# Joining weights of the first three attention pairs brought to the free axis through DRAM, in a hybrid decoder kernel

## The reference

```python
def dilated_attention(q, k, v):
    outs = [dilated_branch(q, k, v, w, d) for (w, d) in DILATED_BRANCHES]
    ms = jnp.stack([m for _, m, _ in outs])      # the maximum of each branch
    ls = jnp.stack([l for _, _, l in outs])      # the sum of its exponentials
    os_ = jnp.stack([o for o, _, _ in outs])
    wts = ls * jnp.exp(ms - jnp.max(ms, axis=0, keepdims=True))
    o = jnp.einsum('gbhs,gbhsd->bhsd', wts, os_) / jnp.sum(wts, axis=0)[..., None]
    return o
```

## Time and profile before

| | |
|---|---|
| median of 3 runs | 2058.66 us |
| the profiled execution | 2058.07 us |
| its span | 2056.3 us |
| PE busy | 2044.2 us, 99% |
| DVE, ACT, POOL busy | 66%, 44%, 44% |
| DMA share of the attention stretch (240 to 440 us) | 0.1 to 0.3 |

### The profile page before, as it was taken

How to read it: one execution, slowest core, us unless ns; L and a number is a source line. 1 busy time by engine, 2 the same in 40 slices (tenths; PEclk the granted TensorE clock), 3 DMA queues, 4 the chain that set the end, 5 groups by cost and what they waited for, 6 DMA issues and landing times.

```text
span 2056.3 us, 26348 instructions
## 1 busy us (share of the span) xinstructions
PE 2044.2 (99%) x10180; PEld 1695.3 (82%) x10180; DVE 1349.2 (66%) x1708; ACT 901.8 (44%) x1268; POOL 898.0 (44%) x467
## 2 busy tenths in 40 slices
PE   9999999999999999999999999999999999999998
PEld 7888888888888888888888888888888888888887
DVE  6668766747866555566999314538756556567987
ACT  4221565825544444443435420225544444454445
POOL 3322122233887777750003423345877877730002
PEclk9999999999999999999999999999999999999999
DMA  5110111133222222129982211113321222249872
GB/s 182 42 62 31 53 44 40 42 124 123 93 93 76 78 93 92 63 93 349 377 306 73 78 36 31 52 41 133 113 93 63 92 92 74 81 153 388 303 281 83
DMA packets 102534, 242.29 MB, mean 118 GB/s; under 512 B 12329, under 2 KB 18826, under 8 KB 102410
## 3 DMA queue, kind: packets, MB, share of 16 engines
q1 hardware_dynamic: 100538, 235.87, 32.3%
q10 hardware_dynamic: 1872, 4.74, 0.6%
HBM read 202.79 MB, written 35.68 MB: 116 GB/s over the span
## 4 chain that ended last, share of the span: by engine, by line
PE 94%; DMA 2%; DVE 1%; SPq 1%; POOL 0%; issue 0%; ACT 0%; POOLq 0%; DVEq 0%
PE ps L1508 13%; PE ps L1506 13%; PE ps L1507 13%; PE ps L991 6%; PE ps L994 6%; PE ps L997 6%; PE ps L1540 6%; PE ps L1542 6%; PE ps L1543 6%; PE ps L1221 2%; PE ps L1223 2%; PE ps L1222 2%; PE ps L1611 1%; PE ps L1613 1%; PE ps L1612 1%; PE ps L1363 1%
## 5 line engine op out<-in xcount | busy, mean ns | idle before, releaser
L696 POOL TENSOR_TENSOR w_hi<-w_raw,ones 128x1024 fp32r<-128x1024 f32 x52 | 103.5, 1990 | 664.5 <-PE ps L997 223.7
L1506 PE MATMUL ps<-t_hi,w_hi 128*128 128x512 f32 x672 | 261.4, 389 | 0.0
L1507 PE MATMUL ps<-t_lo,w_hi 128*128 128x512 f32 x672 | 261.4, 389 | 0.0
L1508 PE MATMUL ps<-t_hi,w_lo 128*128 128x512 f32 x672 | 261.4, 389 | 0.0
L760 POOL TENSOR_TENSOR w_lo<-w_sum,w_hi 128x1024 fp32r<-128x1024 f32 x84 | 248.3, 2958 | 14.1 <-ACT w_hi L2825 14.1
L1540 PE MATMUL ps<-d_hi 128*128 128x512 f32 (+1 forms) x632 | 242.3, 383 | 0.1
L1543 PE MATMUL ps<-d_hi,d_lo 128*128 128x512 f32 (+1 forms) x632 | 241.6, 382 | 0.0
L1542 PE MATMUL ps<-d_lo,d_hi 128*128 128x512 f32 (+1 forms) x632 | 241.6, 382 | 0.0
L760 POOL TENSOR_TENSOR w_lo<-w_raw,w_hi 128x1024 fp32r<-128x1024 f32 x84 | 158.0, 1881 | 159.8 <-ACT w_hi L2825 145.8
L1506 PE MATMUL ps<-act_hi,w_hi 128*128 128x512 f32 x504 | 196.1, 389 | 0.0
L1507 PE MATMUL ps<-act_lo,w_hi 128*128 128x512 f32 x504 | 196.1, 389 | 0.0
(11 more groups left out here) (335 smaller groups left out, 4342.8 us busy)
## 6 DMA issues: line engine op xcount, KB each, us to landing
w_raw<-w_up SPq DMA_DIRECT2D x44, 1024.0 KB, 4.9
d_ring<-w_dn SPq DMA_DIRECT2D x146, 256.0 KB, 7.6
d_ring<-g_kept SPq DMA_DIRECT2D x124, 256.0 KB, 9.1
g_kept<-gst SPq DMA_DIRECT2D x44, 512.0 KB, 3.6
w_raw<-w_in SPq DMA_DIRECT2D x24, 512.0 KB, 3.6
chain_a<-g_kept SPq DMA_DIRECT2D x44, 256.0 KB, 8.6
x_kept<-x SPq DMA_DIRECT2D x16, 512.0 KB, 9.2
x<-x_kept SPq DMA_DIRECT2D x16, 512.0 KB, 9.9
```

Of the source, the lines that this page charges most:

```text
L1506: pe.matmul(out, wh, bh, start=(fresh and j == 0), stop=False, skip_group_check=True)
L1507: pe.matmul(out, wh, bl, start=False, stop=False, skip_group_check=True)
L1508: ins = pe.matmul(out, wl, bh, start=False, stop=(j == 3), skip_group_check=True)
```

## The change

For pairs 0 to 2 the weights `a_part` (16 KB) are written to a DRAM buffer of 32 rows by 128 positions, element by element (one `factors_out` per pair), and read back (`factors_in`, two DMAs per chunk, one for each head of the pair), each row repeated over 64 partitions, into the one buffer `a_rows[0]`. `combine_out` reads that in place of PSUM. `spread` and `factor_transposes` stay for pair 3 alone. The order of the DVE instructions is as before. Core of the diff:

```diff
+        factor_row = [nc.dram_tensor(f"factor_row{i}", (32, P), F32).ap() for i in range(3)]
...
+            def factors_out(hp):
+                sp.wait_ge(A.st, 8 * hp + 8)
+                sp.dma_start(factor_row[hp].rearrange("i p -> p i"), a_part[:].rearrange("p w i -> p (w i)"),
+                             allow_slow_non_contiguous=True).then_inc(A.fw, 16)
+
+            def factors_in(hp, c):
+                which, jb = factor_chunk(c)
+                if c == 0:
+                    sp.wait_ge(A.fw, 16 * hp + 16)
+                if hp or c:
+                    sp.wait_ge(A.cm, factor_done(hp, c - 1) if c else factor_done(hp - 1, 3))
+                for h in range(2):
+                    row = factor_row[hp].rearrange("(w t x) p -> w x t p", w=2, t=4)[which:which + 1, 2 * jb + h]
+                    sp.dma_start(a_rows[0][64 * h:64 * h + 64, :].rearrange("d (t p) -> d t p", p=P),
+                                 row.to_broadcast([64, 4, P])).then_inc(A.fr, 16)
...
                     if (hp, t) in ((0, 0), (1, 2)):
                         spread_outs(hp)
+                    if (hp, t) == (NHP - 1, 0):
+                        factors_out(0)
                     if hp > 1 and t == 0:
                         move_classes(hp - 2)
+                    if (hp, t) == (NHP - 1, 0):
+                        for c in range(3):
+                            factors_in(0, c)
+                    if (hp, t) == (NHP - 1, 1):
+                        factors_in(0, 3)
+            factors_out(1)
             move_classes(NHP - 2)
+            factors_in(1, 0)
             for m in range(KT):
                 plain(N_WO + m, w_out[m])
+                if m == 0:
+                    for c in range(1, 3):
+                        factors_in(1, c)
                 if m == 1:
+                    factors_in(1, 3)
+                    factors_out(2)
+                    factors_in(2, 0)
                     move_classes(NHP - 1)
+                    for c in range(1, 3):
+                        factors_in(2, c)
+                if m == 2:
+                    factors_in(2, 3)
...
-                    if hp and 1 <= s + i < 5:
-                        factor_transposes(hp - 1, s + i - 1)
...
-                if hp == NHP - 1 and s == 1:
-                    factor_transposes(hp - 1, 0)
...
-                if hp and (2 if hp == NHP - 1 else 1) <= s < 5:
-                    factor_transposes(hp - 1, s - 1)
...
-                dve.wait_ge(A.rt, 4 * hp + c + 1)
+                if hp < MOVED:
+                    dve.wait_ge(A.fr, 32 * (4 * hp + c + 1))
+                    factors = a_rows[0][:]
+                else:
+                    dve.wait_ge(A.rt, 4 * (hp - MOVED) + c + 1)
+                    factors = ps[:, factor_bank(hp, c), :]
...
-                if hp and s in (2, 4):
-                    spread(hp - 1, s - 1)
...
-                if hp and s in (0, 2):
-                    spread(hp - 1, s)
...
-                if s == 1:
-                    spread(hp - 1, 0)
...
-                    if 1 <= s < 4:
-                        spread(hp - 1, s)
```

More of the change, by code:

```diff
@@ L304, in __init__ @@
                 self.rt = sem("a_factor_transposed")
+                self.fw = sem("a_factors_in_dram")
+                self.fr = sem("a_factors_read")
                 self.cm = sem("a_out_combined")
@@ L506, in build, with factor_chunk, factor_done @@
         R_F1 = R_WOC + KT
+        def factor_chunk(c):
+            return (1, c) if c < 2 else (0, c - 2)
+        def factor_done(hp, c):
+            return 6 * hp + (1, 2, 3, 5)[c]
         def out_factor(bp, h):
@@ L963, in near_out, with factor_steps @@
             return oT[:, hp if hp else 2, :]
-        def factor_chunk(c):
-            return (1, c) if c < 2 else (0, c - 2)
         def factor_bank(hp, c):
             return (6, 4, 5, 6)[c] if hp == NHP - 1 else 6
+        MOVED = NHP - 1
+        def factor_steps(hp):
+            return hp if hp <= MOVED else MOVED + 5 * (hp - MOVED)
         def factor_rows(hp, c):
             return a_rows[c if hp == NHP - 1 else 0]
-        def factor_done(hp, c):
-            return 6 * hp + (1, 2, 3, 5)[c]
         WO_ORDER = (4, 5, 6, 7, 0, 1, 2, 3)
@@ L1323, in move_statistics @@
                 pe.wait_ge(A.st, 8 * hp + 1)
-                if hp:
-                    pe.wait_ge(A.cm, factor_done(hp - 1, 3))
                 for r in range(4):
@@ L1331, in factor_transposes @@
             def factor_transposes(hp, c):
[L1333 to L1339, removed]
+                pe.wait_ge(A.rb, factor_steps(hp) + c + 2)
+                if c == 3:
                     pe.wait_ge(A.cm, factor_done(hp, 0))
@@ L1998, in statistics_differ @@
                 dve.wait_ge(A.st, 8 * hp + 3)
-                if hp:
-                    dve.wait_ge(A.rb, 5 * hp)
+                if 0 < hp <= MOVED:
+                    dve.wait_ge(A.fw, 16 * hp)
+                elif hp:
+                    dve.wait_ge(A.rb, factor_steps(hp))
                 dve.tensor_tensor(a_part[:], a_least[:, None, :].to_broadcast([P, 2, 16]), both[:, :, :, 0], ALU.subtract
@@ L2006, in statistics_join @@
                 both = a_stat[:, hp % 2]
-                dve.wait_ge(A.rb, 5 * hp + 1)
+                dve.wait_ge(A.rb, factor_steps(hp) + 1)
                 dve.tensor_tensor(a_sums[:], a_part[:], both[:, :, :, 1], ALU.mult).then_inc(A.st, 1)
@@ L2020, in combine_out @@
                 cols = slice(jb * HALF, (jb + 1) * HALF)
-                dve.wait_ge(A.rt, 4 * hp + c + 1)
+                if hp < MOVED:
[4 more added lines that the diff above has]
+                    factors = ps[:, factor_bank(hp, c), :]
                 dve.wait_ge(A.of, SA * (hp + 1))
                 if which:
-                    dve.tensor_tensor(a_far[:, cols], ps[:, factor_bank(hp, c), :], a_far[:, cols], ALU.mult).then_inc(A.cm, 1)
+                    dve.tensor_tensor(a_far[:, cols], factors, a_far[:, cols], ALU.mult).then_inc(A.cm, 1)
                     return
                 out = oT[:, hp, cols]
-                dve.tensor_tensor(out, ps[:, factor_bank(hp, c), :], near_out(hp)[:, cols], ALU.mult).then_inc(A.cm, 1)
+                dve.tensor_tensor(out, factors, near_out(hp)[:, cols], ALU.mult).then_inc(A.cm, 1)
                 dve.wait_ge(A.cm, factor_done(hp, c))
@@ L2654, in spread @@
                 act.wait_ge(A.st, 8 * hp + 8)
-                if hp < NHP - 1 and 4 * hp + c:
-                    act.wait_ge(A.rt, 4 * hp + c)
                 factor = a_part[:, which, :].rearrange("p (t j h) -> p t j h", j=2, h=2)[:, :, jb, :]
```

## The result

The changed kernel takes 2087.88 us (2087.25 to 2090.46, 4 runs) against 2058.64 of the kernel before on the same chip: a ratio of 1.0144 (95% interval 1.0128 to 1.016), 29.2 us slower. 2064.2 us had been predicted. The profiled execution takes 2088.15 us around a span of 2086.3.

What follows compares the result with a forecast made beforehand. PE's own work was taken to bound the kernel: -5.3 us for removed transposes, +9.3 for waits, +1.5 for the clock, so +5.5 us on 2058.66 gives 2064.2 us. The 8-in-10 range was 2058.0 to 2071.0.

Steps and rivals of the forecast that it cites:

- Four times that is 2.6 us, so 2.2 + 2.0 = 4.2 us, which I take: Each pair's scattered store: landing time scaled from a 1024-element row that landed in 2.2 us, taken as 4.2 us.
- twice the time per element: Upper bound for the scattered store's landing: 4.2 + 2.6 = 6.8 us.
- one extra pass: Scattered store: read-modify-write of transfers under 512 bytes, counted as one more time per element, an estimate, giving 6.8 us.
- Pairs 0 and 1: nothing in front of PE: Steps of pairs 0 and 1: store and reads on SP's queue come late for DVE at most, and PE does not wait.
- 6.2 us of cover: Pair 0, chunk 0: DVE stands 2.5 us for the read, covered by its 6.20 us idle before 304.83.
- the output piece: Pair 3's steps: chunk 1 of pair 2, read after 16 class moves, makes PE wait 6.6 us.
- `values(25)`: Late chunk 0 of pair 2 delays DVE's copy, so PE waits 1.6 us here; tops(27) then adds 0.4 us.
- I leave its 0.69 us as it is: DVE's joining multiplications: same places and same length as before, 0.69 us each.
- the scattered store is slow: Rival: from 4.7 us on, pair 2's store delays chunk 0 and class moves, PE one us for each; 2066 to 2071, chance 0.20.
- sign of being wrong: PE waits in pairs 1 or 2, pair 3's stall under 4 us, or clock at 1.00 with time over 2064.
- 10 ns per element and DMA engine: Evidence against a slow scattered store: a row with 0.64 us for 64 elements.
- The clock: The 6.6 us stall lowers PE's clock; PE restarts at half pace, ends 0 and 3 us, taken as 1.5 us.

Runs made afterwards that it cites:

- the run with two pairs: The changed kernel with only pairs 0 and 1 through DRAM by the scattered store, pair 2 by spreads and transposes as before: 2067.08 us, ratio 1.0046.
- `t_more`: Timed transfer added to the kernel before, read by nobody: 1024 single 4-byte elements to DRAM, 32 bytes apart, neighbours from one partition; landed in 4.5 us.
- the quick store: The changed kernel with each store written as 128 rows of 128 bytes instead of 4096 single elements (wrong weights, same instructions): 2063.70 us, ratio 1.0025.
- three-pair version: All three pairs by one PE transpose and a row store, pair 2's reads ahead of and between class moves, against the kernel before: 2055.13 us, ratio 0.9984.
- the run of six transfers: The kernel before with five 16 KB transfers and one of 4 KB between MLP weight loads, each waited for, read by nobody: profiled execution 2058.7 us.

## Why the prediction was wrong, step by step

**The step that failed** is "Four times that is 2.6 us, so 2.2 + 2.0 = 4.2 us, which I take", with its upper bound of 6.8 us. The store lands in 15.1 us, and in pair 0 of the run with two pairs in 16.4. The earlier trace rows show 1024 elements *read* from DRAM; a scattered write to DRAM is another operation. By itself, the same 4096 elements read back took 4.2 and 6.6 us, near what I took; only the write, with its elements 4 bytes apart, takes 15. The bound "twice the time per element" had no row behind it, and I took the fixed part from the reading row too, where 256 elements written in the order of the change already take 7.5 us. The read-modify-write rule that I cited from the Trainium skill ("DMA: Bandwidth & Descriptors") pointed the right way, since small writes were the slow case; its one extra pass, my 6.8 us, was less than half of the price. It says nothing of neighbours, and it cannot tell `t_more` (4.5 us) from the turned store of as many elements (8.4). No run shows the extra pass itself, and the limit of 512 bytes does not show either: rows of 128 bytes landed in the same 1.4 us as rows of 512, and 1024 turned elements 64 bytes apart in 2.4.

**"Pairs 0 and 1: nothing in front of PE" failed with it.** The prediction had the store landed long before the class moves were through at 292.3. A store that takes 16.4 us, as in the run with two pairs, holds the first read until 296.6 by itself. A second effect, which I had at nothing, adds up to 1.8 us: the class moves behind the store are issued in 17.6 us instead of 11.3, and the read goes at 298.4. DVE waits 8.4 us for chunk 0, where 2.5 were forecast and 6.2 us of cover were there. With the quick store DVE waits 2.17 and 2.60 us, and PE 1.5 us in all outside the two waits of pair 2: the cover was judged rightly, the landing of the store was not.

**Pair 2.** The order of waits was right and their sizes follow the store. With a store of 2.5 us PE waits 6.0 us at the output piece (6.6 forecast) and 1.0 at `values(25)` (1.6 and 0.4 forecast), and the total of 2063.70 us lies by the forecast 2064.2. That it comes so close is in part luck. By the prediction's own rule the shorter store takes the 1.6 us at `values(25)` away; the 1.0 us that is there is less than the 1.4 by which the join ran over. "I leave its 0.69 us as it is" was thus a second term put at nothing: the weights now come from SBUF, and the join took 2.12 us. Another 1.5 us of small waits stand where 0.4 and 0.7 were forecast. With 15.1 us the stall moves: chunk 0 now comes last, 12.3 us in one piece, and chunk 1's shrinks to 2.6.

**The rival "the scattered store is slow"** was the right one, with 0.20. It was priced at 10 us at most, "PE by one us for each". Its rule was good for pair 2: from 4.7 us to 15.1 it gives 10.4 us on top of 5.5, so 15.9. It left out pairs 0 and 1, which cost 8.4 us where -3.5 had stood, 11.9 more: 27.8 us together, of 29.2. The prediction's sign of being wrong, waits of PE in pairs 1 or 2, came. "10 ns per element and DMA engine", its evidence against, again came from reads.

**The clock.** Right in kind: it falls to 0.57 in the long wait. At 1.5 us the term fitted the quick store, where waits of 8.5 us less 5.3 leave 1.8 of the measured 5.0. In the changed kernel it is some 8 us (7.7 and 8.5 by the two sums above).

**Right:** the 0.44 us of a call (with the quick store pair 2's weights are written at 385.46, where they were ready at 388.68 before: 3.2 us earlier, 3.5 forecast; eight removed calls are worth 3.6 us where little else is late); reads that land in 2.8 to 4.2 us, 3.0 in the median, where 2.5 was taken; the read behind the class moves as a stall (6.5 us come back when it goes ahead). That ACT's spreads are worth nothing fits every run, but none tested it alone.

**Left open:** why the written elements delay one another; why class moves are issued more slowly behind such a store, and by how much (17.6 and 17.5 us in the changed kernel, 13.4 and 15.4 in the run with two pairs, 12.4 to 13.5 with nobody reading); and what of the three-pair version's gain is real.

## What to carry to other kernels

Price a store by a store: a row of the trace for reading single elements bounds nothing for writing them, and a transposing store to DRAM, whose neighbours come from different partitions, cost over ten times as much as the same bytes in rows (15.2 and 1.4 us). One small transpose on PE ahead of the store makes rows of it. Then look at what the read stands behind in its queue: issuing 16 small transfers takes 11 us, and with two reads behind them this kernel was 6.5 us slower. Last, an operand that moves from PSUM to SBUF can make the instruction that reads it longer: look at what else is at work there.

## What the runs showed of the hardware

- One DMA of 4096 single elements to DRAM lands in 6.3 us with the elements 256 bytes apart, 9.0 at 64, 12.7 at 32, 16.5 at 16 and 17.5 to 19.4 at 8, each partition in its own stretch. Denser is slower there; turned, it takes 8.5 us at 64 bytes and 15.0 at 4. Into SBUF the same number lands in 4.1 us.
- Such a store is still under way when its traffic has ended. In the run of six transfers, the store of the change was issued at 1219.4, the DMA engines moved its last elements by 1229, and it landed at 1234.5.
- SP issues the 16 transfers behind it in 12.4 to 17.6 us instead of 10.2 to 11.7, though each of them is the same as before.
- A multiplication of 128x512 on DVE with both operands in SBUF took 1.60 to 2.12 us in the four places where POOL split a tile, and 0.69 elsewhere; with one operand in PSUM it took 0.69 beside the same work.
- After 12.3 us of waiting the granted clock was 0.58 over the next 10 us, in which PE was busy for 8.9, and 1.00 in the ten behind them. The way back that the prediction had no row for is shown here.
